# The input of a two-layer model kernel fetched already turned, behind the first weight block, and its norm's sums taken over partitions

## The reference, cut to what matters

```python
def rms_norm(x, g):
    xf = x.astype(jnp.float32)
    y = xf * lax.rsqrt(jnp.mean(xf * xf, axis=-1, keepdims=True) + EPS)
    return (y * g.astype(jnp.float32)).astype(x.dtype)

def mamba2_layer(x, norm_g, w_in, conv_w, conv_b, dt_bias, a_log, d_skip, gate_norm_g, w_out):
    h = rms_norm(x, norm_g)
    zxbcdt = h @ w_in
    z = zxbcdt[..., :SSM_D_INNER]
    xbc = zxbcdt[..., SSM_D_INNER:SSM_D_INNER + SSM_CONV_DIM]
    dt_raw = zxbcdt[..., SSM_D_INNER + SSM_CONV_DIM:]
    xbc = jax.nn.silu(causal_depthwise_conv(xbc, conv_w, conv_b))
    dt = jax.nn.softplus(dt_raw.astype(jnp.float32) + dt_bias.astype(jnp.float32)).reshape(b, s, G, R)
    ...
```

## Time and profile before

| what | value |
|---|---|
| time, median of 3 runs | 1220.44 us (1220.33 to 1221.62) |
| time of the profiled execution | 1220.39 us |
| its span | 1218.7 us, so 1.7 us lie around the span |
| TensorE busy | 1206.0 us, 99% of the span |
| DVE, ACT busy | 905.9 us (74%), 668.1 us (55%) |
| chain that ended last | 93% on TensorE |

### The profile page before, as it was taken

How to read it: one execution, slowest core, us unless ns; L and a number is a source line. 1 busy time by engine, 2 the same in 40 slices (tenths; PEclk the granted TensorE clock), 3 DMA queues, 4 the chain that set the end, 5 groups by cost and what they waited for, 6 DMA issues and landing times.

```text
span 1218.7 us, 18050 instructions
## 1 busy us (share of the span) xinstructions
PE 1206.0 (99%) x6649; PEld 1003.5 (82%) x6649; DVE 905.9 (74%) x1399; ACT 668.1 (55%) x1093; POOL 52.1 (4%) x46
## 2 busy tenths in 40 slices
PE   9999999999999999999999999999999999999997
PEld 6788888888888887878787789847889888999886
DVE  5888889888965366677777779998778434786776
ACT  6566756675663244655656473685567321577222
POOL 1011210112010000000000000000000000000000
PEclk9999999999999999999999999999999999999999
DMA  6433333423324332222222233123333332232322
GB/s 173 135 96 118 86 105 103 120 72 116 104 70 135 98 87 87 70 70 69 75 79 70 70 87 87 41 63 106 100 106 105 118 90 76 97 106 96 111 88 102
DMA packets 169099, 115.42 MB, mean 95 GB/s; under 512 B 3392, under 2 KB 162400, under 8 KB 168016
## 3 DMA queue, kind: packets, MB, share of 16 engines
q1 hardware_dynamic: 167152, 104.02, 28.9%
q0 software_dynamic: 1888, 10.62, 2.5%
HBM read 112.46 MB, written 2.16 MB: 94 GB/s over the span
## 4 chain that ended last, share of the span: by engine, by line
PE 93%; DVE 3%; DMA 1%; ACT 1%; issue 1%; SPq 0%; ACTq 0%; DVEq 0%
PE psum L656 53%; PE psum L1189 10%; PE psum L1285 6%; PE psum L926 4%; PE psum L858 4%; PE psum L1032 3%; PE psum L1087 2%; PE psum L895 2%; PE psum L913 1%; PE psum L762 1%; PE psum L770 1%; PE psum L753 1%; PE psum L907 1%; PE psum L744 1%; PE psum L738 1%
## 5 line engine op out<-in xcount | busy, mean ns | idle before, releaser
L1321 ACT ACTIVATE w_hi<-w_raw 128x1024 fp32r<-128x1024 f32 x158 | 167.0, 1057 | 279.9 <-PE psum L656 203.5
L1998 DVE TENSOR_TENSOR w_lo<-w_raw,w_hi 128x1024 fp32r<-128x1024 f32 x158 | 193.1, 1222 | 110.9 <-ACT w_hi L1321 110.2
L656 PE MATMUL psum<-a_hi,w_hi 128*128 128x512 f32 (+1 forms) x656 | 233.4, 376 | 0.2
L656 PE MATMUL psum<-a_lo,w_hi 128*128 128x512 f32 (+1 forms) x656 | 228.6, 368 | 0.0
L656 PE MATMUL psum<-a_hi,w_lo 128*128 128x512 f32 (+1 forms) x656 | 227.8, 367 | 0.0
L656 PE MATMUL psum<-b_hi,w_hi 128*128 128x512 f32 x376 | 150.0, 399 | 0.5 <-DVE w_lo L1998 0.3
L656 PE MATMUL psum<-b_lo,w_hi 128*128 128x512 f32 x376 | 148.6, 395 | 0.0
L656 PE MATMUL psum<-b_hi,w_lo 128*128 128x512 f32 x376 | 148.0, 394 | 0.0
L656 PEld LDWEIGHTS psum<-a_hi,w_hi 128*128 128x128 f32 x656 | 118.3, 188 | 24.7 <-issue 3.9
L656 PEld LDWEIGHTS psum<-a_hi,w_lo 128*128 128x128 f32 x656 | 118.1, 188 | 21.4
L656 PEld LDWEIGHTS psum<-a_lo,w_hi 128*128 128x128 f32 x656 | 118.0, 188 | 19.8
(11 more groups left out here) (398 smaller groups left out, 2506.8 us busy)
## 6 DMA issues: line engine op xcount, KB each, us to landing
w_raw<-a_w_in SPq DMA_DIRECT2D x48, 512.0 KB, 3.9
w_raw<-w_down SPq DMA_DIRECT2D x32, 512.0 KB, 3.8
arena<-acs POOLq DMA_DIRECT2D x8, 1024.0 KB, 4.9
w_raw<-a_w_out SPq DMA_DIRECT2D x16, 512.0 KB, 4.1
w_raw<-w_kv SPq DMA_DIRECT2D x16, 512.0 KB, 3.7
w_raw<-b_w_in SPq DMA_DIRECT2D x16, 512.0 KB, 4.0
w_raw<-w_in SPq DMA_DIRECT2D x14, 512.0 KB, 3.8
arena<-w_up SPq DMA_DIRECT2D x7, 1024.0 KB, 5.3
```

The lines of the kernel that those rows point to most:

```text
L656: ins = mm(out, wv[:, u.par, k, :], xv[:, k0 + k, c0:c0 + cn], start=(first and begin and i == 0 and n == 0), stop=(last and end and i == ...
L1321: ac(w_hi[:, u.par, :, :], w_raw[:, u.par, :, :], ACT.Copy).then_inc(S["hi_ready"], 1)
L1998: tt(w_lo[:, u.par, :, :], w_raw[:, u.par, :, :], f32(w_hi[:, u.par, :, :]), ALU.subtract).then_inc(S["lo_ready"], 1)
```

## The change

- x is given to the kernel turned, and four DMAs bring it straight into `h`. `turn_x`, the copies to `h` and two idle products between them are gone; `a_hi` and `a_lo` are made from `h`.
- SP's order: the norm's gain (`anorm_in`, from POOL to SP), weight block j0, the four pieces of x, block j1, the dt weights, and the identity matrix last.
- The idle products at the start are 13 instead of 4.
- The norm's sums: ACT squares the 8 blocks of `h` into `x_sq`, DVE adds them up in 7 additions, TensorE sums over partitions (`sums`, four small matmuls) behind tile j1, and ACT takes the root from PSUM. So `spread` moves from the middle of j1 to behind the first two feature blocks of j2.
- On DVE, `lo(u + 3)` moves from behind `evacuate_in(g, 1)` to behind `evacuate_in(g, 0)`, and `lo(u + 4)` from behind `evacuate_in(g, 2)` to behind `evacuate_in(g, 1)`.
- j0 to j5 go to PSUM banks 1, 0, 3, 2, 1, 0 instead of 1, 0, 1, 0, 1, 0, so j2 and j3 need not wait for an evacuation.

```diff
+FIRST_BANKS = (1, 0, 3, 2, 1, 0)
+WARM = 13
+SPREAD = 2
...
+            sp.dma_start(par[:, C_ANORM:C_KVN], t["params"][:, C_ANORM:C_KVN]).then_inc(S["anorm_in"], 16)
+            load(Lin(U_MAMBA), t["a_w_in"], 0, ssd_cols(Lin(0))[0])
+            for i in range(4):
+                sp.dma_start(h[:, 2 * i:2 * i + 2, META:T2], t["x_t"].rearrange("(k p) s -> p k s", p=P)
+                             [:, 2 * i:2 * i + 2, :]).then_inc(S[f"x_in{i}"], 16)
+            load(Lin(U_MAMBA + 1), t["a_w_in"], 0, ssd_cols(Lin(0))[1])
+            sp.dma_start(wdt, t["w_dt"]).then_inc(S["raw0"], 16)
             sp.dma_start(ident, t["consts"][:, K_ID:K_ID + P]).then_inc(S["con_in"], 16)
...
-            warm(4).then_inc(S["unit_done"], 1)
-            pe.wait_ge(S["con_in"], 16)
+            warm(WARM).then_inc(S["unit_done"], 1)
...
-            tile_of(u, m, a_hi, a_lo, False, ks=range(2), ready=("x_lo", 1))
-            turn_x(range(6, KT))
-            tile_of(u, m, a_hi, a_lo, False, ks=range(2, KT), ready=("x_lo", 3))
+            tile_of(u, m, a_hi, a_lo, False, ready=("x_lo", 1))
             u, m = u + 1, m + 1
             tile_of(u, m, a_hi, a_lo, False, ks=range(3))
             pe.wait_ge(S["dtw_ready"], 1)
             dt_products()
             tile_of(u, m, a_hi, a_lo, False, ks=range(3, 5))
-            pe.wait_ge(S["rs_ready"], 1)
-            spread(bank(4), stat_at(X_RS), TOKENS1, S["rb_ready"])
             tile_of(u, m, a_hi, a_lo, False, ks=range(5, KT))
+            pe.wait_ge(S["x_cpv"], KT - 1)
+            sums(bank(7), x_sq[:, 0, :], TOKENS1, S["x_tp"])
...
-            first_group(2)
+            first_group(2, range(SPREAD))
+            pe.wait_ge(S["con_in"], 16)
+            pe.wait_ge(S["rs_ready"], 1)
+            spread(bank(4), stat_at(X_RS), TOKENS1, S["rb_ready"])
+            first_group(2, range(SPREAD, KT))
...
+            hi(Lin(U_MAMBA))
             act.wait_ge(S["anorm_in"], 16)
-            turned_high((0, 1))
-            hi(Lin(U_MAMBA))
...
+            turned_high(range(KT))
             hi(Lin(U_MAMBA + 1))
-            turned_copies((3, 5, 7))
-            for i in range(1, NT):
-                token_squares(i)
...
+            for k in range(KT):
+                ac(x_sq[:, k, :], h[:, k, META:T2], ACT.Square).then_inc(S["xsum_ready"], 1)
+            hi(Lin(U_MAMBA + 2))
             own.wait()
-            root(stat_at(X_SD), stat_at(X_SUM), eps1, 1.0 / D, S["xsd_ready"])
-            hi(Lin(U_MAMBA + 2))
+            act.wait_ge(S["x_tp"], 1)
+            root(stat_at(X_SD), bank(7)[:, 0:NT], eps1, 1.0 / D, S["xsd_ready"])
...
+            for k in range(1, KT):
+                dve.wait_ge(S["xsum_ready"], k + 1)
+                if k > 1:
+                    dve.wait_ge(S["x_cpv"], k - 1)
+                tt(x_sq[:, 0, :], x_sq[:, 0, :], x_sq[:, k, :], ALU.add).then_inc(S["x_cpv"], 1)
...
             evacuate_in(g, 0)
+            lo(u + 3)
             time_steps()
             taps_of(g, 0)
             evacuate_in(g, 1)
-            lo(u + 3)
+            lo(u + 4)
             taps_of(g, 1)
             evacuate_in(g, 2)
-            lo(u + 4)
```

More of the change, by code:

```diff
@@ L458, in group @@
                     load(g * 6 + (U_MAMBA + j), t["a_w_in"], 0, c)
-            sp.dma_start(ident, t["consts"][:, K_ID:K_ID + P]).then_inc(S["con_in"], 16)
-            for i in range(4):
-                if i == 1:
-                    load(Lin(U_MAMBA), t["a_w_in"], 0, ssd_cols(Lin(0))[0])
-                if i == 3:
-                    sp.dma_start(wdt, t["w_dt"]).then_inc(S["raw0"], 16)
-                sp.dma_start(x_tok[:, :, 256 * i:256 * i + 256], t["x"].rearrange("(t p) d -> p t d", p=P)
-                             [:, :, 256 * i:256 * i + 256]).then_inc(S[f"x_in{i}"], 16)
-            group(Lin(0), 1)
+            sp.dma_start(par[:, C_ANORM:C_KVN], t["params"][:, C_ANORM:C_KVN]).then_inc(S["anorm_in"], 16)
[5 more added lines that the diff above has]
+            sp.dma_start(wdt, t["w_dt"]).then_inc(S["raw0"], 16)
+            sp.dma_start(ident, t["consts"][:, K_ID:K_ID + P]).then_inc(S["con_in"], 16)
+            group(Lin(0), 2)
             group(Lin(1))
@@ L635, in tile_of @@
             def tile_of(u, m, xh, xl, wide, k0=0, first=True, last=True, ks=range(KT), ready=None,
-                        begin=None, end=None, lo="lo_ready", free=None, mark=None):
+                        begin=None, end=None, lo="lo_ready", free=None, mark=None, out=None):
                 begin = ks[0] == 0 if begin is None else begin
@@ L654, in tile_of @@
                     for n, (wv, xv) in enumerate(((w_hi, xh), (w_hi, xl), (w_lo, xh))):
-                        for out, c0, cn in outs:
-                            ins = mm(out, wv[:, u.par, k, :], xv[:, k0 + k, c0:c0 + cn],
+                        for o, c0, cn in outs:
+                            ins = mm(o, wv[:, u.par, k, :], xv[:, k0 + k, c0:c0 + cn],
                                      start=(first and begin and i == 0 and n == 0),
@@ L687, in _, with dt_products @@
             pe.wait_ge(S["warm_set"], 1)
[L688 to L693 removed]
+            warm(WARM).then_inc(S["unit_done"], 1)
+            def dt_products():
+                for k in range(KT):
                     if k % 2 == 0:
                         pe.wait_ge(S[f"x_in{k // 2}"], 16)
[L696 to L707 removed]
                     c = slice(32 * (k % 4), 32 * (k % 4) + 32)
@@ L803, in first_group @@
             def first_group(j, ks=range(KT)):
-                tile_of(Lin(U_MAMBA + j), Lin(M_MAMBA + j), a_hi, a_lo, False, ks=ks)
+                tile_of(Lin(U_MAMBA + j), Lin(M_MAMBA + j), a_hi, a_lo, False, ks=ks,
+                        free=M_MAMBA if j < 4 else M_MAMBA + j - 3, out=bank(FIRST_BANKS[j]))
             def turn_steps(v, at, ready=None):
@@ L2036, in turned_low @@
                     dve.wait_ge(S["x_hi"], k + 1)
-                    stt(a_lo[:, k, 0:SEQ], bank(2 + k % 6), par[:, C_ANORM + k:C_ANORM + k + 1],
+                    stt(a_lo[:, k, 0:SEQ], h[:, k, META:T2], par[:, C_ANORM + k:C_ANORM + k + 1],
                         f32(a_hi[:, k, 0:SEQ]), ALU.mult, ALU.subtract).then_inc(S["x_lo"], 1)
-            def turned_copies(ks):
-                for k in ks:
-                    dve.wait_ge(S["x_tp"], k + 1)
-                    cp(h[:, k, META:T2], bank(2 + k % 6)).then_inc(S["x_cpv"], 1)
-            turned_low((0,))
-            turned_copies((0,))
-            turned_low((1,))
             lo(Lin(U_MAMBA))
-            turned_low(range(2, KT))
+            turned_low(range(KT))
             lo(Lin(U_MAMBA + 1))
@@ L2059, in _ @@
             own(ts(spl[:, 5, 0:1], par[:, C_SUBG:C_SUBG + 1], 1.0 - LAMBDA_INIT, None, ALU.mult))
-            dve.wait_ge(S["xsd_ready"], 1)
-            nc.vector.reciprocal(stat_at(X_RS), stat_at(X_SD)).then_inc(S["rs_ready"], 1)
             rows = slice(96, 128)
@@ L2068, in _ @@
             lo(Lin(U_MAMBA + 2))
+            dve.wait_ge(S["xsd_ready"], 1)
+            nc.vector.reciprocal(stat_at(X_RS), stat_at(X_SD)).then_inc(S["rs_ready"], 1)
             dve.wait_ge(S["rt_ready"], 1)
@@ L2082, in evacuate_in @@
                 n, m = g * 6 + j, g * 6 + (M_MAMBA + j)
+                v = bank(FIRST_BANKS[j]) if g.reg is None and g.c == 0 else acc(m)
                 if j == 0:
```

52 lines of the change are left out of this document (10 added, 42 removed).

## The result

| what | before | after |
|---|---|---|
| time, median | 1220.38 us (4 runs, 1220.29 to 1221.62) | 1228.84 us (4 runs, 1228.69 to 1229.22) |
| ratio, 95% interval | | 1.0068 (1.0056 to 1.0079): slower |
| time of the profiled execution | 1220.39 us | 1229.22 us |
| its span | 1218.7 us | 1227.6 us |

The forecast was 1227.6 us in 1225.0 to 1230.4. The changed kernel is slower by 8.5 us, or 0.7%. Five more executions of it, taken later, gave a median of 1227.80 (1227.43 to 1229.45); why they spread is part of the story.

What follows compares the result with a forecast made beforehand. TensorE, busy 99%, bounds the kernel, with DVE right behind in the first group. Start 1.3 and transposes about 1.0 gained; waits 0.8, sums 0.97, j4 3.6, j5 3.85 lost: +6.9, rest rounding; 1220.4 + 7.2 = 1227.6 us, range 1225.0 to 1230.4.

Steps and rivals of the forecast that it cites:

- main case: First group: DVE's waits for high parts delay TensorE, j5 starts 7.3 us later; 1225.8 to 1228.8 us, chance 0.65.
- three signs of being wrong: In the changed profile: DVE's two waits shorter, TensorE's matmuls at half speed after a wait, or TensorE regaining time in the second group.
- This comes to nothing: Start: an earlier clock rise could let j0 start at 8.5 instead of 10.0, without gain, because j1 waits for its block.
- rival of late transfers: Start: x in 2 KB pieces slows the queue, block j1 lands 1 to 2 us late; about 1229.2 us, chance 0.07.
- The two moved low parts: DVE, j3 and j4: waits of 1.8 and 3.8 us for ACT's high parts; TensorE waits 0.6 and 3.6 us.
- The wait before j5: TensorE ahead of j5: low part ends at 50.65, wanted at 46.85, a wait of 3.85 us.
- The clock: Rival, TensorE: the clock falls in one of the two waits near 4 us; up to 2.7 us lost, 1230.3, chance 0.13.
- if it fell in the first wait, the slack before the second would take it: Clock falling in the wait before j4: the slack before j5 absorbs it; in the second wait up to 2.7 us are lost.
- No row shows a clock that fell: Argument against the clock falling in TensorE's waits: no trace row shows a fall; that rival's chance was 0.13.
- The table load: ACT, chain to j4's high part: the load takes the row's 1.28 us, without the skill's further 1380 ns of draining.
- its 1229.0: Total if ACT's table load takes the skill's page total: both late low parts 1.4 us later, against 1227.6 by the row.

Runs made afterwards that it cites:

- before_lo: The kernel before with only the two low parts of j3 and j4 moved as in the change: 1224.48 us, ratio 1.0041.
- lo_back: The changed kernel with the low parts of j3 and j4 back at their old places on DVE: 1223.25 us, ratio 1.0028.
- hi_early: The changed kernel with ACT's high part of j4 ahead of the first tap of j1 and the silu of j0: 1225.90 us, ratio 1.0048.
- fill_j4: The changed kernel with seven idle products ahead of j4 alone: 1229.08 us, ratio 1.0074.
- fill_j5: The changed kernel with four idle products ahead of j5 alone: 1227.90 us, ratio 1.0063.
- after_again: The changed kernel itself run once more, with no edit, five times: 1227.80 us, ratio 1.0068 against the kernel before.
- keep_clock: The changed kernel with 7 idle products ahead of j4 and 7 ahead of j5: 1227.57 us, ratio 1.0061.
- lo_back_fill: lo_back with five idle products ahead of j3: 1222.05 us, ratio 1.0015.
- es_back: The changed kernel with both low parts back, the sums inside j1 and the spread directly ahead of j2: 1220.60 us, ratio 1.0004.

## Why the prediction was right, and what it missed

The forecast, 1227.6, was 1.2 under the first median and 0.2 under that of the later runs, and the side was right. The mechanism of its main case was right, and a term was missing from its sum. One of its own three signs of being wrong came: "TensorE's matmuls go at half speed after a wait". The first median, 1228.84, lies at the very edge of its main case (1225.8 to 1228.8). How near the number came is in part luck, since it depends on how the clock falls in an execution.

| step of the prediction | predicted | measured |
|---|---|---|
| idle products end, j0 starts | 10.0 | 10.05 |
| squares and additions hidden under j1, end | 22 | 21.67 |
| j1 starts | 16.2 | 16.11 |
| sums start (behind j1 and the dt products) | 23.8 | 23.84 |
| evacuation of j0 | 28.1 | 27.93 |
| DVE waits for the high part of j3, of j4 | 1.8, 3.8 | 1.83, 3.77 |
| j3 starts, after a wait of | 31.9, 0.6 | 31.82, 0.51 |
| j4 starts, after a wait of | 41.2, 3.6 | 41.10, 3.46 |
| j5 starts, after a wait of | 50.7, 3.85 | 50.60, 2.11 |
| clock behind the waits | no term | fell twice, 1.53 lost in j5 |

**The start.** "This comes to nothing" held. In the traces of the new start with its 13 idle products, these ended between 8.9 and 10.4 and j0 started between 8.7 and 10.1, but j1 always at 15.65 to 16.28. The last transfer before j1 let ACT start at 13.64, for 13.9 in the prediction, so its rival of late transfers did not come.

**The two moved low parts.** Right in place and size. before_lo and lo_back show the mechanism from both sides, and hi_early that it runs through ACT.

**The wait before j5** was shown as 2.11 and not 3.85. That is no error of DVE's chain, whose low part ended at 50.45 (predicted 50.65). TensorE arrived late, because j4 ran partly at half clock. In fill_j4, where j4 ran at full clock, the wait is 3.69. In the prediction's sum the parts come to 6.9, the start of j5 is put 7.3 later, and the last line adds 7.2; measured are 7.23.

**The clock** is the term that was missing from the sum. It stood as a rival, with a chance of 0.13, and this rival was right in mechanism and even in its split: "if it fell in the first wait, the slack before the second would take it" is what fill_j5 shows. Its price, up to 2.7, holds as an upper bound: the fall in j5 cost 1.53 in the first profile (5.48 for 3.95) and 1.41 in fill_j4, and j4 lost 2.6 in after_again (8.02 for 5.41 in fill_j4), which the wait behind it took up. Its chance was too low, and the one reason against it was misread. "No row shows a clock that fell" holds for the rows that the prediction shows, but not for the trace of the kernel before. TensorE is idle there from 1212.3 to the end of the span at 1218.7, and the granted clock fell in that pause (window, busy time and count, clock, DMA share, GB/s):

```profile
1212.00:1213.00 1.00, 0.28 (x2) 1.00 0.77 283
...
1215.00:1216.00 1.00, 0.00 (x0) 0.83 0.97 358
1216.00:1217.00 1.00, 0.00 (x0) 0.50 1.02 383
```

No matmul comes behind it, so it cost nothing and gave no price; but it was there as a sign. Once TensorE works, its longest wait before that pause is 1.7 us, and the prediction expected 3.6 and 3.85; that the clock did not fall in the shorter ones was no evidence. The Trainium skill (TensorE: Matmul & The Clock Gate, Part 1, What's actually happening) said that an idle array goes back to half its clock, and the six profiled executions with a wait of 3.46 to 3.69 in the first group agree. 1220.39 + 7.23 + 1.61 = 1229.23, for 1229.22 in the profiled execution, is only bookkeeping with measured numbers: it says that nothing more is lost behind 56 us. Of the 1.61 the clock is 1.53; the rest is that the first half of j5 takes 3.95 instead of 3.87 without any fall.

**The table load.** The row has 1.28, and silu starts at 38.12, right behind it. The Trainium skill (ScalarE: Activation LUTs, What ACT_TABLE_LOAD costs) adds some 1380 ns of draining; this chain does not show them. The median would fit its 1229.0 too, which is a warning: the place decides, and the low part of j4 came at 40.96 and not 1.4 later.

**Where the 8.5 us are.** From the medians: 5.5 from the moved low parts (keep_clock over lo_back_fill, 1227.57 - 1222.05), 1.3 from the clock (the changed kernel over keep_clock), 1.45 from that part of the norm's delay which the earlier sums and spread take away (lo_back_fill over es_back, 1222.05 - 1220.60), and 0.4 from all the rest of the new start (es_back over the kernel before). The sum is 8.6. The 0.4 is not distinct from nothing, and in es_back the evacuation of j0 is still 1.4 later than in the kernel before (26.15 for 24.76). The 1.3 hangs on which executions fall into the median: it is 1.2 with the median of all nine times of the changed kernel, 1228.76, and 0.2 with that of the later five.

## What to carry to other kernels

When an instruction moves ahead on an engine that works in order, list what its input still has to pass through at the new place. If the work that it was moved past was the time in which another engine made that input, the move turns it into a wait, and all that is queued behind pays. A wait of TensorE can have a second price, the clock behind it: here all unfilled waits of 3.46 to 3.69 us had it and some of 2.1 to 2.9 us. It is paid only where no other wait follows that takes it up. And if the times of a kernel spread over 2 or 3 us, as lo_back's did, look for such a wait before taking a difference of medians as the cost of an edit.
